# Gate spreading in a PEER layer: one-hot rows built by one-input comparisons on VectorE alone

## The reference

```python
expert_idx = take_along_axis(cand_i, best_pos)          # (512 tokens, 128 slots), value = row * 128 + col
gates = softmax(best_s, axis=-1)                        # one gate per slot
act = gelu(einsum('td,ted->te', xb, u[ib]))             # u, v: 16384 experts x 1024
out = einsum('te,ted->td', gb * act, v[ib])
```

## Time and profile before

| | us |
|---|---|
| median of three runs | 2559.25 |
| lowest, highest | 2556.57, 2559.41 |
| span of the profiled execution, first to last instruction | 2554.5 |
| TensorE busy | 2194.6 (86%) |
| VectorE busy | 1572.2 (62%) |
| ScalarE busy | 722.2 (28%) |
| GpSimd busy | 346.7 (14%) |

### The profile page before, as it was taken

How to read it: one execution, slowest core, us unless ns; L and a number is a source line. 1 busy time by engine, 2 the same in 40 slices (tenths; PEclk the granted TensorE clock), 3 DMA queues, 4 the chain that set the end, 5 groups by cost and what they waited for, 6 DMA issues and landing times. The chain is left out here.

```text
span 2554.5 us, 30718 instructions
## 1 busy us (share of the span) xinstructions
PE 2194.6 (86%) x10156; PEld 1798.1 (70%) x10156; DVE 1572.2 (62%) x2745; ACT 722.2 (28%) x1007; POOL 346.7 (14%) x233
## 2 busy tenths in 40 slices
PE   5997687887796046669999999999999999999997
PEld 3876465775674045558888888888888888888886
DVE  4426343523399999995555566655556665555565
ACT  4312572333231035552222222222222222222222
POOL 0000010102242269980000000000000000000000
PEclk9996688898898589999999999999999999999999
DMA  4310002312130023334333333333333333333331
GB/s 146 100 33 1 1 1 82 132 66 66 51 139 25 0 99 132 132 159 147 116 117 117 117 116 109 114 110 117 117 117 117 113 111 111 113 117 117 117 117 65
DMA packets 103269, 247.52 MB, mean 97 GB/s; under 512 B 7968, under 2 KB 57520, under 8 KB 101808
## 3 DMA queue, kind: packets, MB, share of 16 engines
q1 hardware_dynamic: 103216, 246.84, 29.0%
HBM read 213.25 MB, written 33.55 MB: 97 GB/s over the span
## 5 line engine op out<-in xcount | busy, mean ns | idle before, releaser
L1517 PE MATMUL bank<-xs_hi,u_lo 128*128 128x512 f32 x1024 | 399.0, 390 | 3.3 <-DVE u_lo L1603 3.3
L1518 PE MATMUL bank<-xs_lo,u_hi 128*128 128x512 f32 x1024 | 399.1, 390 | 0.0
L1519 PE MATMUL bank<-xs_hi,u_hi 128*128 128x512 f32 x1024 | 399.0, 390 | 0.0
L1535 PE MATMUL bank<-v_hi,w_lo 128*128 128x512 f32 x1024 | 398.3, 389 | 0.0
L1536 PE MATMUL bank<-v_lo,w_hi 128*128 128x512 f32 x1024 | 398.3, 389 | 0.0
L1537 PE MATMUL bank<-v_hi,w_hi 128*128 128x512 f32 x1024 | 398.3, 389 | 0.0
L1572 ACT ACTIVATE gel<-bank 128x512 f32<-128x512 f32 x128 | 76.7, 599 | 1060.8 <-PE bank L1519 1060.8
L1618 DVE TENSOR_TENSOR gel<-gel,gates 128x128 f32<-128x128 f32 x128 | 37.5, 293 | 544.2 <-ACT gel L1572 544.2
L1636 DVE TENSOR_TENSOR y<-y,bank 128x512 f32<-128x512 f32 x512 | 337.6, 680 | 5.4 <-PE bank L1537 5.4
L1401 POOL TENSOR_TENSOR hot<-hot,slot_t 128x384 f32<-128x384 f32 x128 | 224.9, 1793 | 22.9 <-DVE hot L1385 22.9
L1385 DVE TENSOR_TENSOR hot<-iota,slot_t 128x1024 f32<-128x1024 f32 x128 | 224.8, 1833 | 3.7 <-PEq L1132 3.7
(11 more groups left out here) (328 smaller groups left out, 2936.9 us busy)
## 6 DMA issues: line engine op xcount, KB each, us to landing
raw<-in_u_tiles SPq DMA_DIRECT2D x128, 512.0 KB, 3.2
raw<-in_v SPq DMA_DIRECT2D x128, 512.0 KB, 4.4
w_raw<-in_w_tiles SPq DMA_DIRECT2D x80, 512.0 KB, 4.5
g_in<-gate_scratch SPq DMA_DIRECT2D x128, 192.0 KB, 4.4
h<-in_x SPq DMA_DIRECT2D x4, 512.0 KB, 5.6
h_scratch<-h SPq DMA_DIRECT2D x1, 2048.0 KB, 8.6
xf_scratch<-xf_hi SPq DMA_DIRECT2D x1, 2048.0 KB, 13.0
xf_scratch<-xf_lo SPq DMA_DIRECT2D x1, 2048.0 KB, 17.3
```

What stands on the lines that cost most here:

```text
L1517: nc.tensor.matmul(bank, u_lo[:, k % 2, c, :], xs_hi[:, c, :], start=(c == 0), stop=False)
L1518: nc.tensor.matmul(bank, u_hi[:, k % 2, c, :], xs_lo[:, c, :], start=False, stop=False)
L1519: last = nc.tensor.matmul(bank, u_hi[:, k % 2, c, :], xs_hi[:, c, :], start=False, stop=(c == DC - 1))
L1535: nc.tensor.matmul(y, w_lo[:, e, tk], v_hi[:, e, f], start=(e % 2 == 0), stop=False)
```

## The change

The one `tensor_tensor` of a batch becomes eight `tensor_scalar` instructions on VectorE of 128 elements per partition each. Each reads `iota` as its one tensor input and compares it with one column of `slot_t` as a per-partition scalar, whose address is computed from the loop variable. The four that make the column matrices carry a second per-partition scalar, the gate, by which they multiply in the same instruction. GpSimd has no work left in the stage. ScalarE only reads the banks. TensorE waits for `hot_ready`, which VectorE's eighth instruction raises.

```diff
-                    nc.vector.tensor_tensor(
-                        hot[:, b], iota.unsqueeze(1).unsqueeze(1).to_broadcast([P, 2, NT, P]),
-                        slot_t[:, 0:2, bass.ds(token(c, i, b), NT)].unsqueeze(3).to_broadcast([P, 2, NT, P]),
-                        ALU.is_equal).then_inc(hot_ready, 1)
+                    for k in range(NT):
+                        at = bass.ds(token(c, i, b) + k, 1)
+                        nc.vector.tensor_scalar(hot[:, b, 0, k, :], iota, slot_t[:, 0, at], None, ALU.is_equal)
+                        last = nc.vector.tensor_scalar(hot[:, b, 1, k, :], iota, slot_t[:, 1, at], slot_t[:, 2, at],
+                                                       ALU.is_equal, ALU.mult)
+                    last.then_inc(hot_ready, 1)
...
-        @block.gpsimd
-        def _(pool):
...
-                        pool.wait_ge(hot_ready, batch(c, i, b) + 1)
-                        o = hot[:, b, 1, 0:NPOOL, :]
-                        nc.gpsimd.tensor_tensor(o, o, slot_t[:, 2, bass.ds(token(c, i, b), NPOOL)].unsqueeze(2).
-                                                to_broadcast([P, NPOOL, P]), ALU.mult).then_inc(gated_pool, 1)
...
-                    pe.wait_ge(gated_pool, n + 1)
-                    pe.wait_ge(gated_act, n + 1)
+                    pe.wait_ge(hot_ready, n + 1)
...
-            def gate(c, i, b):
...
-                act.wait_ge(hot_ready, batch(c, i, b) + 1)
-                for k in range(NPOOL, NT):
-                    o = hot[:, b % HOT, 1, k, :]
-                    last = nc.scalar.activation(o, o, ACT.Identity, scale=slot_t[:, 2, bass.ds(token(c, i, b) + k, 1)])
-                last.then_inc(gated_act, 1)
...
-                with act.Fori(0, TBODIES - (c == TB - 1)) as i:
-                    body(c, i)
-            body(TB - 1, TBODIES - 1, last=True)
+                with act.Fori(0, TBODIES) as i:
+                    for b in range(HOT):
+                        read(c, i, b)
```

More of the change, by code:

```diff
@@ L1322, in layer @@
     NT, HOT = 4, 4
-    NPOOL = 3
     TD = TB - 1
@@ L1335, in layer @@
     hot_ready, hot_used, g_read = sem("hot_ready"), sem("hot_used"), sem("g_read")
-    gated_pool, gated_act = sem("gated_pool"), sem("gated_act")
     u_hi_done, u_lo_done, v_hi_done, v_lo_done = (sem(x) for x in ("u_hi_done", "u_lo_done", "v_hi_done", "v_lo_done"))
@@ L1392, in _ @@
                     body(c, i)
-        @block.gpsimd
-        def _(pool):
-            for c in range(TB):
-                with pool.Fori(0, TBODIES) as i:
-                    for b in range(HOT):
-                        pool.wait_ge(hot_ready, batch(c, i, b) + 1)
-                        o = hot[:, b, 1, 0:NPOOL, :]
-                        nc.gpsimd.tensor_tensor(o, o, slot_t[:, 2, bass.ds(token(c, i, b), NPOOL)].unsqueeze(2).
-                                                to_broadcast([P, NPOOL, P]), ALU.mult).then_inc(gated_pool, 1)
         @block.tensor
@@ L1436, in read @@
                                      ACT.Identity).then_inc(g_read, 1)
[L1438 to L1443, removed]
             for c in range(TB):
```

## The result

The kernel became slightly slower: 2562.6 us (median of 17 runs) against 2556.78 (17 runs), a ratio of 1.0021 with a 95% interval of 1.0014 to 1.0029, or some 5.4 us. I had forecast 20 us less than before, 2538.8. That the time lies in the stated range of 2526 to 2573 says little for the forecast: the range had been drawn wide enough to take in rival A, and the sign was wrong.

What follows compares the result with a forecast made beforehand. VectorE and GpSimd, slowing each other, bound the spreading stage. Eight instructions at 0.201 us over 128 batches (205.8 us) plus a 2.0 us tail give 207.8 against 228.3, 20.5 less: 2538.8 us from 2559.25, range 2526 to 2573.

Steps and rivals of the forecast that it cites:

- rival A: VectorE's column comparisons: second scalar fetched after the first, 1.868 us a batch, kernel 12.8 us slower at 2572; chance 0.20.
- What bounds the kernel: Spreading stage: VectorE and GpSimd, slowing each other, busy 224.8 and 224.9 of 228.3 us; pitch 1.766 us per batch.
- the one-to-one passage of the stage's time: Spreading stage to kernel end: the stage's gain or loss, forecast 20.5 us less, is the kernel's, one to one.
- First piece: Elements on VectorE: one-input fp32 instructions take two per cycle, so 128 elements cost 0.067 us.
- Second piece: Fixed part on VectorE: 0.069 us with constants, 0.134 with a per-partition scalar; one-scalar comparison of 128 elements 0.201 us.
- Third piece: Second scalar in four of the eight VectorE instructions: between nothing and 0.065 us; taken as nothing, latencies overlapping.
- turning point: VectorE's column comparisons: change becomes a loss when a batch passes 1.768 us, a second scalar of 0.040 us.
- Rival B: VectorE's sequencer becomes the bound, gate address needing a register instruction: 1.73 us a batch, kernel about 2554; chance 0.14.
- Rival C: VectorE's short instructions: scalars cost nothing, fetched during the one ahead; 0.136 us each, kernel 2472; chance 0.08.
- rival D: VectorE's comparisons by address pass one element per cycle: 0.267 us each, batch 2.14, kernel 47 slower, 2606; chance 0.05.
- The contention: Spreading stage: GpSimd and VectorE lengthen each other's instructions (comparison 1218 to 1843 ns); GpSimd's departure ends it; no separate size.
- The signs in the profile: Profile after: row and column comparisons both near 0.29 us recorded, 0.35 for columns under rival A; TensorE waiting 0.4 us.

Runs made afterwards that it cites:

- the first two experiments: Changed kernel, column comparison without its gate scalar and multiplication: one run, 2536.95 us; then multiplying by constant 0.5 instead of the gate: ratio 0.9904 to the kernel before.

## Why the prediction was wrong

**What bounds the kernel, and the one-to-one passage of the stage's time: right.** Stage +5.3 us, span +5.1, ratio 5.4 us. The stores landed in 21.7 to 22.7 us as before, 420 us of the expert stage again had TensorE busy in 420.

**First piece, two elements per cycle: right.** The constants-only comparison of 128 elements came at 0.135 us where 0.136 was worked out.

**Second piece, a one-scalar comparison: right, 0.196 for 0.201 us.** The 0.40 us of line 287 is the one pitch of a pair (0.401 by the records), so the first behind a stop, and a first pitch is longer than those behind it: in the changed kernel's stage the first is 0.202 us and the median 0.196, in the stage without GpSimd 1.142 and 1.135. Line 1689 seemed to confirm the 0.134, but its sum gives 0.137 and not 0.135, and with the 1.066 us that 1024 elements take by the pitches of the runs it gives 0.130. The 0.005 too much, 1024 times, are 5 us.

**Third piece, the second scalar: this is the step that failed.** I bounded it between nothing and 0.065 us and put it at nothing, with the argument that a fixed part of 0.13 "looks like a latency, and two latencies of one instruction can overlap". They do not: the second scalar measured 0.060 us on top of the first one's 0.061, by the pitches with a constant and with a scalar in memory (0.196 and 0.256). The rows had only shown that a latency is not hidden behind the instruction ahead, which speaks against overlap, and I used them for it. It added 512 x 0.060 = 30.7 us; less the 5.1 us of the second piece, that is 25.6 of the 25.8 us between the 20.5 saved by forecast and the 5.3 lost.

**Rival A: right in mechanism and place, its price too high.** It gave 1.868 us a batch for 1.808 measured and 12.8 us for 5.4, since it carried the 0.005 eight times and another 0.005 on the second scalar four times. Its turning point, a second scalar of 0.040 us at 0.201 for the first, was the useful number: the range of the unknown lay on both sides of it, so that a chance of 0.20 on A was low for what the rows had shown.

**Rival B, the sequencer: fell.** Its records grew to 93 ns, and when the gate's computed address was taken away they were 57 ns and the time stayed. **Rival C** (0.136 us) and **rival D** (0.267) fell with the pitch of 0.196.

**The contention: right, but not priced.** I named the slowing by GpSimd and let it vanish inside the sum. Had the 81 us been set against the new instructions, it would have been plain that the change swaps one large saving for one large cost, and that a form which keeps the saving without the scalars was near.

**The signs in the profile.** The recorded durations that I named (0.29 us, and 0.35 for the second under A) hold only at the start of the stage, where they are 0.28 and 0.34; they moved through it (below). Their difference stayed at 0.06 us and did point at A. The pitch was the sign to name. TensorE waited 0.65 us a batch for VectorE, not 0.4, and GpSimd had its 128 instructions fewer.

## What to carry to other kernels

Each per-partition scalar that a VectorE instruction reads from memory costs its pitch some 0.06 us, one after the other (seen on 128 and on 1024 elements), and two elements per cycle win back only 0.067 us on 128 elements. A two-input comparison of 128 elements had a pitch of 0.202 us (line 1389 of the version with three gates on ScalarE), a one-scalar comparison 0.196. So many short one-input instructions win nothing over one long two-input instruction, since each pays its scalar and a fixed 0.07 us (0.135 - 0.067) again: four row comparisons at 0.784 us against 0.602 for one of 512. When two engines slow each other, measure each alone first, since what contention costs (here 81 us) is what a cheaper repair can aim at. When an unknown cost's bounds straddle the point at which the sign flips, the forecast's sign is open, and the chances should say so.

## What the runs showed that I had not expected

In these streams of short instructions the recorded duration grows from start to end of the stage while the pitch stays. Line 1385 of the changed kernel, of the one with a fixed gate address, and of the one with constants only:

```profile
L1385 DVE TENSOR_SCALAR hot<-iota,slot_t x512: 280/421/573, 913.2 to 1144.0; 128x128 f32<-128x128 f32 x171
```

```profile
L1385 DVE TENSOR_SCALAR hot<-iota,slot_t x512: 283/706/1067, 913.2 to 1143.6; 128x128 f32<-128x128 f32 x171
```

```profile
L1385 DVE TENSOR_SCALAR hot<-iota x512: 221/459/701, 917.9 to 1055.8; 128x128 f32<-128x128 f32 x171
```

The ends keep the work's pace. From the recorded end of the last comparison to the end of the last bank read 1.94 us pass in all three kernels, whether that record lasts 0.63, 1.13 or 0.70 us. So recorded starts run ahead of the work, by up to 0.8 us at the end of the stage, and pitches from starts are too short by a very little: by ends a batch of the changed kernel takes 1.809 us, not 1.806 (means). The growth differs between kernels: in the first two experiments, where every comparison reads one scalar, line 1385 grows only from 278 to 355 and from 282 to 355 ns. With two-input instructions in between it is no larger: 332 to 396 ns for line 1388 of the version with the rows in one comparison, 334 to 360 ns for line 1395 of the version with two gates on ScalarE. Why the records drift was not tested and stays open.
